# Spreading the merge chain's steps over ticks by weights, asking earlier for a group's inputs, and ranking the second tile in fewer ticks

## The chip, the cores and the metric

The kernel runs on one core of a Trainium2 chip. The metric is the device time of one execution in microseconds, as the median of several runs. The engines are TensorE (PE; its weight loads are PEld), VectorE (DVE), ScalarE (ACT), GpSimd (POOL) and the queue of SyncE (SP), which here only issues transfers.

## What is computed

One layer of an encoder over nine tiles of 128 tokens (eight of a prompt, one of eight short samples), all in float32. The part that matters here comes after the attention:

```python
def merge(o_sb, o_sw, o_mem, gates, w_o_sb, w_o_sw, w_o_mem, w_out):
    mixed = (gates[..., 0, :] * (o_sb @ w_o_sb) + gates[..., 1, :] * (o_sw @ w_o_sw)
             + gates[..., 2, :] * (o_mem @ w_o_mem))
    return mixed @ w_out

def peer_block(xb, w_q, pk_keys, u_tab, v_tab):
    q = (xb @ w_q).reshape(t, PEER_HEADS, 2, PEER_DHALF)
    s = jnp.einsum('thpd,hpkd->thpk', q, pk_keys).astype(jnp.float32)
    v1, i1 = lax.top_k(s[:, :, 0], PEER_TOPK)
    v2, i2 = lax.top_k(s[:, :, 1], PEER_TOPK)
    ...
    best, flat = lax.top_k(cand, PEER_TOPK)
    ...
    g = jax.nn.softmax(best, axis=-1)
    a = jax.nn.gelu(jnp.einsum('thkd,td->thk', u_tab[idx], xb))
    return jnp.einsum('thk,thkd->td', (g * a).astype(xb.dtype), v_tab[idx])

    x = x + merge(o_sb, o_sw, o_mem, gates, w_o_sb, w_o_sw, w_o_mem, w_out)
    x = x + peer_ffn(rmsnorm(x, norm_ffn), w_peer_q, peer_keys, peer_u, peer_v)
```

Every token picks 16 of 16384 experts in each of 8 heads: 128 experts a token, 128 "slots" a tile.

## The kernel before

Projection and attention fill the first 850 us and stay as they are. The function `experts` does the rest. Its tiles are in three **groups**, `GROUPS = ((0, 1), (2, 3, 4, 5), (6, 7, 8))`.

**The slots.** Seven tiles (`SEQ = (0, 1, 2, 4, 6, 7, 8)`) have their experts fetched row by row. A slot is one indirect gather by POOL (L1458) of one expert row a token into a ring of nine buffers: 8 KB a token (u and v), or 4 KB (u alone, `u_rows`) for tile 1. DVE forms the dot product with the token (L1996), ACT the GELU and the weight (L1751, L1760) and a folded diagonal matrix (`diag`, L1769), and PE adds the weighted v row into its accumulator (L1654). For one slot in four of the first tile ACT and POOL do that (L1775, L1482). For tile 1 nothing is accumulated: POOL writes the weight to a table in HBM (`gates_scratch`, L1471), which a dense pass at the end uses. Tiles 3 and 5 go by that table too. POOL may refill a ring buffer only when its slot is done (for tile 1, when DVE has formed the dot product).

**Ticks.** Two slots are one tick, 64 ticks are one tile, and ticks 0 to 447 run through the seven tiles: tile 0 has ticks 0 to 63, tile 1 has 64 to 127, tile 2 has 128 to 191. Since each tick has two dot products on DVE, a moment of the trace is turned into a tick by counting them (all on L1996).

**The front.** Beside the slots every engine works off a chain of numbered steps, the "front" of a group: 24 units of merge (PE: gate matmul L1522 and value matmul L1532, in `Y` parts; ACT tanh L1685; DVE product and sum L1905 to L1909, called a mix here), then the output projection (PE L1547, DVE L1917), the norm, transposes (L1557), queries (PE L1570, ACT L1706), scores (PE L1584, ACT L1719 to L1724) and, for the group's first tile, the ranking by DVE (`top`, L1805 to L1847, three pieces a head, the third a long one). The class `Front` gives each kind of work its step numbers; `paces()` says how many steps every engine does at each tick. The step numbers set only the order within an engine; semaphores hold what belongs together. The steps of group 1 have ticks 26 to 123, those of group 2 have 128 to 251, both spread evenly.

**Order within a tick.** DVE does the two dot products, then the tick's steps, then a piece of ranking of another tile (`RANKED`) and the addition of equal experts (`merge` on DVE, L1872 to L1881, `MERGED`, for tiles 1, 3 and 5). ACT does the weights and diagonals, then the steps. PE accumulates, then does the steps. POOL does its two gathers, then, from tick 73 on, four scatters in four of every eight ticks (`SPREAD`, third entry). SP isn't held to ticks: it runs ahead until a semaphore stops it.

**Ranking of tile 1.** `RANK_AT[1] = (30, 48)`: the 24 pieces of tile 1 begin at tick 30 and have 48 ticks; its duplicates are added at ticks 57 to 60 and 81 to 84, which follow from the same two numbers.

## Time and profile before

| | us |
|---|---|
| median of 3 runs | 4054.19 |
| the three runs | 4054.07, 4062.14, 4054.19 |
| profiled execution, device time | 4089.85 |
| profiled execution, span of its trace | 4088.0 |
| PE busy | 3374.4 (83%) |
| DVE busy | 2752.4 (67%) |
| POOL busy | 1625.1 (40%) |
| ACT busy | 1009.5 (25%) |
| all transfers | 1248.31 MB, mean 305 GB/s |

PE is the busiest engine over the whole, but a mean over stages with different limits says little. The first 850 us are projection and attention; ticks begin at 1054 us, tick 26 is at 1222 us, tick 64 at 1463 us, tick 128 at 1867 us, tick 256 at 2673 us; the dense pass begins at tick 282. In an answer of the trace the number in square brackets, or after the bar, is the time that the engine sat idle before the instruction, and what ended it. The trace counts two records for one float32 matmul.

### The profile page before, as it was taken

To read this page: it belongs to the slowest core of one execution; us is meant where nothing else is said; L and a number is where in the kernel's file an instruction comes from. 1 tells how busy PE (TensorE), PEld (TensorE's weight loads), DVE (VectorE), ACT (ScalarE), POOL (GpSimd) and SP (SyncE) were. 2 spreads that over 40 slices of the span, in tenths; PEclk is the share of its full clock that TensorE was granted. 3 is DMA by queue.
4 is the path that set the end of the run, shared out by engine and by line. 5 is a ranking of instruction groups with operands and counts; after the bars stand their busy time and mean duration, and the time that the engine had idled before them with its cause. 6 is when DMAs were issued, how large, how long until landed. Compare 5 with 4: busy or idle time off the path is not lost.

```text
span 4088.0 us, 40853 instructions
## 1 busy us (share of the span) xinstructions
PE 3374.4 (83%) x13885; PEld 1890.4 (46%) x13885; DVE 2752.4 (67%) x5752; ACT 1009.5 (25%) x2925; POOL 1625.1 (40%) x1327
## 2 busy tenths in 40 slices
PE   8999898989759997865979878720989999989998
PEld 4545665578423335432333433210555555555554
DVE  2131456611787786676988799779976888866667
ACT  2111557711333321312222232311111111111111
POOL 0000000000455557757557676776333333333332
PEclk9999889999879998887989989865999999999999
DMA  5911320034899976758989999999999999999998
GB/s 184 301 41 52 127 88 22 14 134 152 332 389 407 365 282 245 249 198 347 412 350 393 413 379 348 362 386 359 415 414 414 405 408 414 411 414 411 414 410 353
DMA packets 320096, 1248.31 MB, mean 305 GB/s; under 512 B 40320, under 2 KB 134784, under 8 KB 216064
## 3 DMA queue, kind: packets, MB, share of 16 engines
q0 software_dynamic: 141312, 872.69, 53.9%
q1 hardware_dynamic: 129408, 347.85, 22.6%
q10 hardware_dynamic: 49168, 25.17, 2.1%
q8 instruction: 110, 1.80, 0.2%
...
HBM read 1190.33 MB, written 56.16 MB: 305 GB/s over the span
## 4 chain that ended last, share of the span: by engine, by line
PE 25%; DVE 24%; DMA 17%; issue 5%; POOL 4%; ACT 2%; another core or an unknown queue 1%; SPq 0%; DVEq 0%; ACTq 0%; POOLq 0%
DMA shared<-in_experts_dram 10%; PE ps L1616 8%; DVE ring L1996 8%; PE ps L1522 5%; PE ps L1605 3%; DMA ring<-in_experts_dram,idx 3%; PE ps L1654 3%; DVE o_x L1968 3%; PE ps L1547 2%; PE ps L1532 2%; DMA shared<-gates_scratch 2%; POOL gates_scratch L1471 2%; POOL ring L1458 2%; DMA s<-s_scratch 1%
## 5 line engine op out<-in xcount | busy, mean ns | idle before, releaser
L1458 POOL DMA_INDIRECT ring<-in_experts_dram,idx x768 | 956.8, 1246 | 1787.3 <-DVE o_x L1968 774.2
L1616 PE MATMUL ps<-shared 128*128 128x512 f32 x1536 | 692.0, 601 | 86.4 <-DMA shared<-in_experts_dram 75.6
L1996 DVE CUSTOM_DVE_ANT_0 ring<-ring,xp 128x1024 f32<-128x1024 f32 x512 | 634.4, 1272 | 126.8 <-DMA ring<-in_experts_dram,idx 86.9
L1751 ACT ACTIVATE act_<-hid 128x2 f32<-128x2 f32 x448 | 91.0, 203 | 2138.7 <-DVE hid L1996 2012.6
L1654 PE MATMUL ps<-ring,diag 64*64 64x512 f32 x2816 | 409.6, 696 | 243.9 <-ACT diag L1769 216.0
L1605 PE MATMUL ps<-shared 128*128 128x256 f32 x2048 | 467.1, 381 | 150.7 <-ACT shared L1737 145.2
L1605 PEld LDWEIGHTS ps<-shared 128*128 128x128 f32 x2048 | 391.1, 191 | 260.8 <-issue 205.5
L1968 DVE SCALAR_TENSOR_TENSOR o_x<-ring,wgt,o_x 128x1024 f32<-128x1024 f32 x384 | 491.7, 1280 | 0.1
L1616 PEld LDWEIGHTS ps<-shared 128*128 128x128 f32 x1536 | 290.1, 192 | 423.0 <-issue 405.9
L1996 DVE CUSTOM_DVE_ANT_0 ring<-ring,mixn 128x1024 f32<-128x1024 f32 x384 | 469.6, 1223 | 18.4 <-DMA ring<-in_experts_dram,idx 15.2
L1522 PE MATMUL ps<-shared 128*128 128x256 f32 (+2 forms) x1152 | 411.7, 506 | 38.8 <-DMA shared<-hT_scratch 29.8
L1522 PEld LDWEIGHTS ps<-shared 128*128 128x128 f32 x1152 | 219.9, 196 | 237.2 <-issue 159.9
L1471 POOL DMA_INDIRECT gates_scratch<-gd,spot x256 | 296.3, 1158 | 78.5 <-issue 77.7
L1654 PEld LDWEIGHTS ps<-ring,diag 64*64 64x64 f32 x2816 | 100.5, 148 | 483.6 <-ACT diag L1769 272.5
L319 PE MATMUL ps<-shared,hT 128*128 128x512 f32 (+1 forms) x720 | 284.9, 551 | 1.8 <-DVE mhT L435 1.3
L1570 PE MATMUL ps<-shared 128*128 128x256 f32 (+2 forms) x768 | 274.6, 510 | 8.9 <-ACT gt L1706 3.7
L1947 DVE TENSOR_TENSOR shared<-shared 128x256 f32<-128x256 f32 x128 | 54.1, 423 | 271.5 <-DMA shared<-gates_scratch 270.7
L1760 ACT ACTIVATE wgt<-act_,gw 128x1 f32<-128x1 f32 x896 | 215.2, 287 | 15.8
L1570 PEld LDWEIGHTS ps<-shared 128*128 128x128 f32 x768 | 148.4, 200 | 146.4 <-issue 110.4
L1532 PE MATMUL ps<-o_x,shared 128*128 128x256 f32 (+2 forms) x576 | 204.6, 495 | 0.6 <-DMA o_x<-o_scratch 0.6
L319 PEld LDWEIGHTS ps<-shared,hT 128*128 128x128 f32 x720 | 134.4, 191 | 131.3 <-issue 125.0
L1458 POOL DMA_INDIRECT ring<-in_u_rows_dram,idx x128 | 143.2, 1119 | 118.1 <-DVE hid L1996 73.8
...
## 6 DMA issues: line engine op xcount, KB each, us to landing
shared<-in_u_blocks_dram SPq DMA_DIRECT2D x128, 512.0 KB
shared<-in_experts_dram SPq DMA_DIRECT2D x128, 512.0 KB
...
shared<-gates_scratch SPq DMA_DIRECT2D x128, 192.0 KB
...
```

The lines of the kernel that those rows point to most:

```text
L319: last = nc.tensor.matmul(ps[:, bank(u), 0:n], src[:, k, t * P:(t + 1) * P], w[:, c % 2, k, 0:n], start=(k == 0), stop=(k == KC - 1))
L1458: i = nc.gpsimd.indirect_dma_start(out=row, out_offset=None, in_=A["u_rows"] if valued(j) else A["experts"], in_offset=bass.IndirectOffset ...
L1471: i = nc.gpsimd.indirect_dma_start(out=G_d.rearrange("e (t o) -> (e t) o", o=1), out_offset=bass.IndirectOffsetOnAxis(ap=spot[:, a, j:j + ...
L1522: last = nc.tensor.matmul(ps[:, 4 + u % 2, 0:N].rearrange("p (i t) -> p i t", t=P), w[:, k * P:(k + 1) * P], hx[:, 0:n, k, :], start=(k == ...
L1532: last = nc.tensor.matmul(ps[:, 6 + u % 2, 0:N].rearrange("p (i t) -> p i t", t=P), w[:, k * P:(k + 1) * P], o[:, 0:n, b, k - KC, :], star ...
L1570: last = nc.tensor.matmul(ps[:, 4 + x % 2, 0:N].rearrange("p (i t) -> p i t", t=P), w[:, c:c + P], hx[:, 0:n, k, :], start=(k == 0), stop= ...
L1605: last = nc.tensor.matmul(ps[:, 2 + b % 2, 0:ND * P].rearrange("p (a t) -> p a t", t=P), du[:, b % 3, k, :], hx[:, 0:ND, k, :], start=(k = ...
L1616: last = nc.tensor.matmul(ps[:, BANKS[a] + h, :], given, dv[:, v % 3, h * HB:(h + 1) * HB], start=False, stop=(b == NK - 1), skip_group_ch ...
L1654: last = nc.tensor.matmul(acc[c * HD:(c + 1) * HD, r, :], diag[rows, (by_pe(j) - 1) % 4, :], ring[rows, j % RING, DM + c * HB:DM + (c + 1) ...
L1760: last = nc.scalar.activation(wgt[:, i:i + 1], act_[:, i:i + 1], ACT.Copy, scale=gw[:, n % 2, i:i + 1])
L1968: last = nc.vector.scalar_tensor_tensor(out=x1, in0=ring[:, j % RING, DM:2 * DM], scalar=wgt[:, j % SLOTS:j % SLOTS + 1], in1=x1, op0=ALU. ...
L1996: last = nc.vector.tensor_tensor_reduce(out=u, in0=u, in1=rows, scale=1.0, scalar=0.0, op0=ALU.mult, op1=ALU.add, accum_out=hid[:, j % SLO ...
```

## The change

Three things. `LEADS = (0, 2, 6)` puts two empty steps before the units of group 1 and six before those of group 2; SP's requests for the group's inputs stand at step 0 as before. `weight()` gives every step of groups 0 and 1 a weight by its kind (a unit part of group 1 has 2.67, an output step 3.6, a query part 4.8), and `spend` hands out the steps of group 1 to ticks by these weights; group 2 is the last one and has weight 1.0 for all steps. `RANK_AT[1]` becomes (28, 34): tile 1 is ranked at ticks 28 to 61, and its duplicates are added at ticks 48 to 51 and 65 to 68.

```diff
--- before.py
+++ after.py
@@ -1010,6 +1010,9 @@
     return PE_UPTO[j + 1]
 
 
+LEADS = (0, 2, 6)
+
+
 class Front:
 
 
@@ -1019,14 +1022,15 @@
         self.cols = n * P
         self.units0, self.tiles0 = 3 * KC * g, sum(len(x) for x in GROUPS[:g])
         self.outs0, self.q0, self.s0 = 4 * self.tiles0, 2 * PH * g, PH * g
-        self.out_at = 3 * KC * Y + 3
+        lead = self.lead = LEADS[g]
+        self.out_at = lead + 3 * KC * Y + 3
         ends = [self.out_at + 3 * n + i for i in range(n)]
         self.q_at = ends[-1] + 10
         soon = 2 if g == 0 else 0
         self.steps = self.q_at + 4 * PH + 12
-        self.unit = {u * Y + y: (u, y) for u in range(3 * KC) for y in range(Y)}
-        self.tanh = {u * Y + Y + 1: u for u in range(3 * KC)}
-        self.mix = {u * Y + Y + 2: u for u in range(3 * KC)}
+        self.unit = {lead + u * Y + y: (u, y) for u in range(3 * KC) for y in range(Y)}
+        self.tanh = {lead + u * Y + Y + 1: u for u in range(3 * KC)}
+        self.mix = {lead + u * Y + Y + 2: u for u in range(3 * KC)}
         self.out = {self.out_at + i: (i // n, i % n) for i in range(4 * n)}
         self.res = {self.out_at + i + 2: (i // n, i % n) for i in range(4 * n)}
         self.square, self.mean, self.root, self.norm, self.turn, self.keep = (
@@ -1045,6 +1049,19 @@
         self.far = tuple(range(self.base + 2, self.base + n))
         self.far0 = PH * sum(len(x) > 2 for x in GROUPS[:g])
 
+    def weight(self, tau):
+        if self.final:
+            return 1.0
+        if tau < self.lead:
+            return 3.0
+        if tau in self.unit:
+            return 8.0 * self.n / self.Y / 3
+        if tau in self.out:
+            return 3.6
+        if tau in self.query:
+            return 1.2 * self.n
+        return 3.5 if tau >= self.q_at else 1.5
+
 
 FRONTS = [Front(g) for g in range(len(GROUPS))]
 FIRST_OF = {f.base: f for f in FRONTS}
@@ -1075,19 +1092,24 @@
     total = [sum(f.steps for f in FRONTS[:g + 1]) for g in range(len(GROUPS))]
     done = FRONTS[0].first_head
     out = [done]
-    start, mid = done, total[0]
-    for i in range(2 * NB):
-        if i < RANK_LEAD:
-            to = start + -(-(mid - start) * (i + 1) // RANK_LEAD)
-        else:
-            to = min(total[1], mid + -(-(total[1] - mid) * (i + 1 - RANK_LEAD) // (2 * NB - 4 - RANK_LEAD)))
+
+    def spend(f, at, first, last):
+        weights = [f.weight(tau) for tau in range(f.steps)]
+        reached = [sum(weights[:tau + 1]) / sum(weights) for tau in range(f.steps)]
+        for i in range(first, last):
+            share = min(1.0, (i + 1 - first) / (last - 4 - first))
+            yield at + sum(x <= share + 1e-9 for x in reached)
+
+    start = done
+    for i in range(RANK_LEAD):
+        to = start + -(-(total[0] - start) * (i + 1) // RANK_LEAD)
         out.append(to - done)
         done = to
-    mid = done
-    for i in range(2 * NB, DENSE_AT):
-        to = min(total[2], mid + -(-(total[2] - mid) * (i + 1 - 2 * NB) // (G2_TICKS - 4)))
-        out.append(to - done)
-        done = to
+    for f, first, last in ((FRONTS[1], RANK_LEAD, 2 * NB), (FRONTS[2], 2 * NB, 4 * NB)):
+        for to in spend(f, total[f.g - 1], first, last):
+            out.append(to - done)
+            done = to
+    out.extend([0] * (DENSE_AT - 4 * NB))
     ticks = len(SEQ) * NB - DENSE_AT
     for i in range(ticks):
         to = total[2] + -(-DENSE_STEPS.steps * (i + 1) // ticks)
@@ -1098,7 +1120,7 @@
 
 PACES = paces()
 
-RANK_AT = {1: (30, 48), 3: (2 * NB + 2, 28), 4: (2 * NB + 34, 28), 5: (2 * NB + 66, 28), 7: (4 * NB + 8, 36), 8: (5 * NB + 6, 48)}
+RANK_AT = {1: (28, 34), 3: (2 * NB + 2, 28), 4: (2 * NB + 34, 28), 5: (2 * NB + 66, 28), 7: (4 * NB + 8, 36), 8: (5 * NB + 6, 48)}
 RANKED = {at + length * c // (3 * PH): (m, c // 3, c % 3) for m, (at, length) in RANK_AT.items() for c in range(3 * PH)}
 SHIFTED, EXPOSED, WEIGHED = ({at + length * (i + 1) // 2 + lag: (m, 4 * i, 4 * i + 4) for m, (at, length) in RANK_AT.items() for i in range(2)}
                              for lag in range(3))
```

What stands on which tick follows from the tables:

| | before | changed |
|---|---|---|
| group 1, unit parts | ticks 26 to 81 | ticks 27 to 74 |
| group 1, output projection (PE) | 83 to 92 | 75 to 85 |
| group 1, transposes | 94 to 96 | 86 to 87 |
| group 1, queries | 98 to 116 | 88 to 116 |
| group 1, ranking of tile 2 | 103 to 121 | 96 to 121 |
| tile 2's experts chosen and weighed | 122 | 123 |
| tile 1, ranked | 30 to 77 | 28 to 61 |
| tile 1, duplicates added | 57 to 60, 81 to 84 | 48 to 51, 65 to 68 |
| group 2, unit parts | 128 to 190 | 133 to 194 |
| group 2, queries | 213 to 240 | 215 to 241 |
| tile 6's experts chosen and weighed | 250 | 251 |

**PE at the start of group 1.** The row with x64 or x72 is accumulation of tile 0 up to tick 26; in the changed kernel L1654, L1522 and L1532 are L1676, L1544 and L1554. Before:

```order
L1654 MATMUL ps<-ring,diag 64x512 x64
L1522 MATMUL ps<-shared 128x512 x6
L1654 MATMUL ps<-ring,diag 64x512 x8
L1522 MATMUL ps<-shared 128x512 x2
L1532 MATMUL ps<-o_x,shared 128x512 x4
L1654 MATMUL ps<-ring,diag 64x512 x4
```

Changed:

```order
L1676 MATMUL ps<-ring,diag 64x512 x72
L1544 MATMUL ps<-shared 128x512 x3
L1676 MATMUL ps<-ring,diag 64x512 x4
L1544 MATMUL ps<-shared 128x512 x5
L1554 MATMUL ps<-o_x,shared 128x512
L1676 MATMUL ps<-ring,diag 64x512 x8
```

The first unit (12 matmuls) begins one tick later, with one part where there were two, and later units come closer together.

**DVE at the last unit of group 1.** Before, ticks 82 and 83 (L1996 is a dot product, L1872 to L1881 add duplicates, L1907 and L1909 are the mix of the last unit):

```order
L1996 ISA ring,hid<-ring,xp 128x1024
...
L1877 TENSOR_TENSOR work<-number 128x1024
L1879 TENSOR_TENSOR work<-work,raw 128x1024
L1880 TENSOR_REDUCE partf<-work 128x16
...
L1996 ISA ring,hid<-ring,xp 128x1024
...
L1907 SCALAR_TENSOR_TENSOR gt<-gt,ps 128x512
L1909 TENSOR_TENSOR mixn<-mixn,gt 128x512
```

Changed, tick 74 and the start of 75 (L2018 is the dot product, L1929 and L1931 the mix):

```order
L2018 ISA ring,hid<-ring,xp 128x1024
L2018 ISA hid 128x1
L1929 SCALAR_TENSOR_TENSOR gt<-gt,ps 128x512
L1931 TENSOR_TENSOR mixn<-mixn,gt 128x512
L2018 ISA ring,hid<-ring,xp 128x1024
```

The additions of duplicates no longer stand between the last units' mixes; they stand at ticks 65 to 68, where mixes of earlier units are.

## Rows read from the trace of the kernel before

**Rows 1.** The page's slices, 102 us each: busy tenths, and GB/s of all transfers

```profile
PE   8999898989759997865979878720989999989998
DVE  2131456611787786676988799779976888866667
POOL 0000000000455557757557676776333333333332
```

**Rows 2.** Windows (stretch, length, busy and count by engine, granted clock, DMA share, GB/s)

```profile
1225.00:1463.00 238.00, 222.04 (x798) 81.47 (x795) 180.67 (x382) 72.17 (x198) 128.50 (x90) 0.97 0.95 372
1463.00:1557.00 94.00, 93.14 (x240) 40.00 (x238) 73.87 (x179) 21.10 (x67) 59.05 (x49) 1.00 0.72 255
1557.00:1578.00 21.00, 0.42 (x1) 0.45 (x2) 18.18 (x30) 2.74 (x10) 16.43 (x16) 0.53 1.02 404
1664.00:1803.00 139.00, 128.92 (x368) 63.31 (x368) 95.93 (x274) 27.46 (x90) 90.91 (x86) 0.96 0.65 223
1803.00:1867.00 64.00, 10.75 (x32) 7.13 (x32) 42.22 (x112) 13.68 (x44) 33.18 (x29) 0.59 0.65 234
1867.00:2673.00 806.00, 639.05 (x3176) 277.94 (x3176) 672.68 (x1777) 222.00 (x743) 551.84 (x491) 0.90 0.96 379
```

**Rows 3.** Waits, 1225 to 1463 us: who waited for whom, us, times, longest

```profile
POOL ring L1458 <- PE ps L1654: 83.0, 29, 6.5
DVE gt L1907 <- ACT gt L1685: 35.2, 7, 8.7
PE ps L1654 <- ACT diag L1769: 16.0, 7, 5.4
```

**Rows 4.** PE's timeline at tick 26 (start, length, line, shapes, count, idle before)

```profile
1223.27 1.98 PE L1654 MATMUL ps<-ring,diag 64*64 64x512 f32 x8 [1.05 <-ACT diag L1769]
1225.18 6.46 PE L1522 MATMUL ps<-shared 128*128 128x512 f32 x12
```

**Rows 5.** PE's timeline around the last unit of group 1, ticks 80 to 83

```profile
1545.68 7.03 PE L1522 MATMUL ps<-shared 128*128 128x512 f32 x16
1552.55 3.60 PE L1532 MATMUL ps<-o_x,shared 128*128 128x512 f32 x8
1577.58 2.90 PE L1547 MATMUL ps<-shared,mixn 128*128 128x256 f32 x6 [21.44 <-DVE mixn L1909]
```

**Rows 6.** DVE's timeline, ticks 81 to 83

```profile
1561.35 1.22 DVE L1879 TENSOR_TENSOR work<-work,raw 128x1024 f32<-128x1024 f32 x1
...
1568.30 1.22 DVE L1877 TENSOR_TENSOR work<-number 128x1024 f32<-128x1024 f32 x1
...
1576.03 0.68 DVE L1907 SCALAR_TENSOR_TENSOR gt<-gt,ps 128x512 f32<-128x512 f32 x1
1576.74 0.69 DVE L1909 TENSOR_TENSOR mixn<-mixn,gt 128x512 f32<-128x512 f32 x1
```

**Rows 7.** Groups of POOL, 1517 to 1709 us (count, busy, mean ns, idle before)

```profile
L1458 POOL DMA_INDIRECT ring<-in_u_rows_dram,idx x64 | 74.3, 1161 | 26.3 <-issue 17.6 <-DVE hid L1996 8.7
L1471 POOL DMA_INDIRECT gates_scratch<-wgt,spot x64 | 73.8, 1154 | 19.5 <-issue 18.9 <-ACT wgt L1760 0.6
```

**Rows 8.** Waits of POOL, 1709 to 1860 us

```profile
POOL ring L1458 <- DVE hid L1996: 48.7, 15, 9.3
```

**Rows 9.** POOL's timeline: start of the scatters, one gather alone, two beside dot products

```profile
1516.93 0.94 POOL L1458 DMA_INDIRECT ring<-in_u_rows_dram,idx  x1 [1.81 <-DVE hid L1996]
...
1840.13 0.94 POOL L1458 DMA_INDIRECT ring<-in_u_rows_dram,idx  x1 [0.30 <-issue]
...
1857.68 2.00 POOL L1458 DMA_INDIRECT ring<-in_u_rows_dram,idx  x1 [0.31 <-DVE hid L1996]
1859.98 1.96 POOL L1458 DMA_INDIRECT ring<-in_experts_dram,idx  x1 [0.30 <-DVE hid L1996]
```

**Rows 10.** DVE's timeline: the first dot product of tick 128

```profile
1867.01 1.23 DVE L1996 CUSTOM_DVE_ANT_0 ring<-ring,xp 128x1024 f32<-128x1024 f32 x1 [2.14 <-DMA ring<-in_experts_dram,idx]
```

**Rows 11.** DVE's timeline: a long ranking piece of tile 1, first and last row, next dot

```profile
1308.04 0.41 DVE L1814 TENSOR_TENSOR work<-v 128x256 f32<-128x256 f32 x1
...
1316.27 1.23 DVE L1996 CUSTOM_DVE_ANT_0 ring<-ring,xp 128x1024 f32<-128x1024 f32 x1
```

**Rows 12.** PE's timeline, end of group 1 and start of group 2

```profile
1814.89 3.44 PE L1584 MATMUL ps<-shared,gt 128*128 128x128 f32 x16 [12.44 <-ACT gt L1706]
1848.13 2.29 PE L1522 MATMUL ps<-shared 128*128 128x384 f32 x3 [29.80 <-DMA shared<-hT_scratch]
```

**Rows 13.** Groups of PE, 1578 to 1664 us, and 1664 to 1867 us

```profile
L1547 PE MATMUL ps<-shared,mixn 128*128 128x256 f32 x256 | 62.4, 403 | 24.9 <-DVE mixn L1909 21.4 <-issue 3.3
...
L1570 PE MATMUL ps<-shared 128*128 128x512 f32 x256 | 116.4, 612 | 7.3 <-ACT gt L1706 3.7 <-issue 2.4 <-ACT shared L1700 1.2
```

## The prediction

> **What bounds the kernel now.** I read the page's slices first, then windows cut where the work of group 1 changes, then in each window who waits for whom, and last the timelines of the engine that nobody keeps waiting. The slices [rows 1] show PE near full from slice 13 on, but a mean hides which engine is late, and the change touches only ticks 26 to 251 (1222 to 2673 us), so the reading stays there.
>
> Ticks 26 to 81 are TensorE's. In 1225 to 1463 it is busy for 222.0 of 238 us and in 1463 to 1557 for 93.1 of 94 [rows 2]; POOL waits 83.0 us there for PE's accumulation, and DVE waits 35.2 us for a tanh that itself waits for PE [rows 3]. PE waits only 16.0 us for diagonals. DVE's idle time in this stretch is slack.
>
> Then PE stands still for 21.4 us [rows 5]: the output projection at tick 83 needs the last unit's mix, which DVE does only after its dot products and two additions of duplicates at ticks 81 and 82 [rows 6]. From tick 73 (1517 us) another engine is late too: POOL does 64 gathers and 64 scatters from 1517 to 1709 us with 8.7 us of waiting for dots [rows 7]. Ticks 98 to 117 (1664 to 1803 us) are PE's again, 128.9 us busy of 139 [rows 2]: eight heads' queries are squeezed into 19 ticks. POOL gets time to spare (48.7 us of waits for dots [rows 8]). What follows, 1803 to 1867 us, is a tail: PE busy 10.8 us, DVE 42.2, POOL 33.2 of 64 [rows 2]. From 1867 to 2673 us, PE, DVE and the transfers are all near full (639, 673 of 806 us, DMA share 0.96) [rows 2].
>
> **The change, group 1.** No instruction is added or taken away; everything is order. Work it out from 1222 us, where tick 26 begins in both.
>
> Start. The two empty steps take no wait away: the inputs are there when PE comes, since it goes from its accumulation straight into the first unit with no idle time noted [rows 4]. So PE starts two parts late: x12 records in 6.46 us now, which move behind the next tick's accumulation. PE loses 6 to 7 us, bounded by zero (if the next ticks come so much sooner) and by 9 (three parts).
>
> Units. A unit costs PE 7.03 + 3.60 us, 10.3 us from start to start where nothing comes between [rows 5]. Between 1225 and 1463 us, 38 ticks, PE accumulates for the rest of its time, about 1.5 us a tick. Before, 1.75 of a unit's four parts stand on a tick: 4.6 + 1.5 = 6.1 us a tick (measured 238 / 38 = 6.3). Changed it is 2 parts: 5.2 + 1.5 = 6.7. The sum over all 24 units is the same, and PE is the bound in both, so the last unit ends at 1556 + 7 = 1563 us, but at **tick 74, not 81**. DVE must keep up. Its ranking of tile 1 now has 34 ticks for 24 pieces instead of 48; a head is about 8.2 us for the long piece [rows 11] and some 3 us for two short ones. Ticks 28 to 63 thus get about a third more of it, 27 us, on top of 180.7 busy us in 238 [rows 2]. With 6.7 us a tick that is about 5.5 on average, under PE's 6.7. I cost it at nothing: what covers it is DVE's wait for tanh [rows 3]. If that cover fails, see the third rival.
>
> The stall. The duplicates are done by tick 68 and the last mix stands directly behind the dot products of tick 74. Tanh and mix are about 2 us (two DVE rows of 0.7 us [rows 6] and one ACT row), so 21.4 us of PE idle time shrink to 3 to 5. Were PE still the bound, that would be a gain of 17 us less the 7 us of the start. But what is late next is POOL.
>
> POOL. Its scatters stay on ticks 73 and later, and by the structure of units DVE reaches tick 73 when unit 21 is done by PE and mixed: 1563 - 20.6 + 6 = 1548 us, where it was 1517 [rows 9]. From there to the gather of tile 2's first slot POOL has 206 transfers (half and half, the number between 1517 and 1860 us). In its full stretch one takes (74.3 + 17.6 + 73.8 + 19.5) / 128 = **1.45 us**, issue time included [rows 7]. So 206 x 1.45 = 298 us, to 1846; 7 us from issue to the dot product, as now (1859.98 to 1867.01 [rows 9, 10]), make 1853. Waits of POOL come on top: between 0 and the 57 us that it has now (8.7 + 48.7 [rows 7, 8]). I take 6, near the lower end, because what makes them now is gone: the queries get 28 ticks instead of 19, in which DVE has 28 x 2.4 + 8 x 11.5 = 160 us of dots and ranking, PE 116.4 + some 18 us [rows 13], and POOL 120 x 1.45 = 174 us. POOL is the largest of the three, if not by much. The first dot product of tick 128 comes at **1859 instead of 1867 us: 8 us sooner**.
>
> Does PE hold this? 1563 + 4, output projection 62.4 us [rows 13], some 16 us for norm and transposes, 134 for queries and scores: 1779, before tick 117 by POOL's clock. Yes.
>
> **The change, group 2.** In the kernel before, the first part of unit 0 waits 29.8 us for its inputs, but nobody waits for PE then: it had run ahead of the ticks, and its accumulation of tick 128 comes only after the dots at 1867 us [rows 10, 12]. So the six empty steps remove a wait that costs nothing. They give ticks 128 to 132 less PE work (5 us each of transfers and dots go on) and put 146 steps where 140 were: 1.22 a tick instead of 1.17, 0.05 x 2.7 = 0.1 us of PE a tick, in a stretch where PE is busy 79% [rows 2]. From 0 to 6 us lost; up to 5 gained if the ring refills sooner at tick 128. I take zero. Tile 6's experts are ready one tick later, at 251, where POOL asks for them after PE has accumulated slot 503 of the same tick, so after DVE has done it. Zero. From tick 256 on nothing is moved.
>
> **A rule weighed.** POOL's gather takes 0.94 us alone and 2.00 or 1.96 beside dot products that follow each other closely [rows 9]. The Trainium skill, GPSIMD Engine Reference, Specifications, says that GpSimd shares its SBUF interface with VectorE and is held up by VectorE instructions with two SBUF inputs, as a dot product is. The trace agrees. Taken to its end for a POOL that never rests, 41% of its transfers (2.44 us of dots in a tick of 5.9) at 2.0 us and the rest at 0.95 would be 1.38 + 0.30 us, 206 of them 346 us, and tick 128 would come 40 us later than forecast. But the 128 transfers of [rows 7] lived beside just that share of dots and had a mean of 1.16; the measurement decides, and 1.45 stands.
>
> **Rivals.**
> 1. *POOL is quicker.* Beside light DVE work a transfer is 0.94 + 0.30 us [rows 9], and the mean from 1709 to 1860 us is (151 - 48.7) / 78 = 1.31. At 1.35, 206 take 278 us, and the gain is 25 or more: 4029. For it: DVE's ranking reads mostly one input. Against: dots come as densely as in [rows 7].
> 2. *POOL keeps waiting.* If DVE's long pieces still come in clumps, POOL's waits are 15 to 20 us, not 6, and tick 128 stays where it is: 4054 to 4058. For it: DVE's 160 us and POOL's 174 are close, and the ring holds only four ticks.
> 3. *DVE stalls PE in ticks 28 to 74, slower.* In twelve units instead of eight tanh and mix stand on the same tick, and DVE must wait there for ACT, which waits for PE, before it does the dots that PE's next accumulation needs. With a long piece in between: 2.4 + 1.4 + 8.2 = 12 us, and 3 us to the diagonals, against 6.7 us of PE work a tick. PE's waits for diagonals, 16.0 us now [rows 3], would grow by up to 4 us for each of eight long pieces. Every microsecond delays tick 73 and with it the whole chain of POOL. It decides from 8 us on (no gain left); at 24 us the time is 4070.
> 4. *Group 2 pays.* The units squeezed into fewer ticks run into a stretch in which three resources are nearly full; 10 us are lost there: 4064 without the gain of group 1, 4056 with it.
>
> **How the numbers follow.** The profiled span is 4088.0 us; the change makes it 4080. The median of the runs shown is 4054.19, 0.8% lower; 8 us less of it is 4046. A measurement of this kernel can tell about 0.2% (8 us) from no change, so this forecast sits on that edge. Chances: forecast 0.45 (own range 4038 to 4054; 0.27 of it under 4046), rival 1 0.17 (4029), rival 2 0.15 (4056), rival 3 0.15 (4070), rival 4 0.08 (4064). Faster 0.27 + 0.17 = 0.44, within 0.2% 0.18 + 0.15 = 0.33, slower 0.23. The range 4022 to 4070 leaves out the far part of rival 1 and the worse half of rival 3.
>
> **What would show it.** Last unit's value matmul of group 1 ending at 1558 to 1568 us (right), later than 1575 (rival 3, with PE's waits for diagonals over 25 us before it). Idle time of PE before the output projection 3 to 5 us. The first scatter near 1550 us. From there to 1855 POOL's waits for dots under 10 us and 1.45 us a transfer; over 20 us of waits is rival 2, under 1.38 us a transfer rival 1. First dot of tick 128 at 1859. From there to tick 256, 806 us as before; 812 or more is rival 4. Tick 256 to the end unchanged (1415 us). I'd be wrong in the mechanism if POOL were idle for long in ticks 76 to 120.

## The result, and the profile after

| | before | changed |
|---|---|---|
| median, us | 4054.09 (5 runs, 4050.39 to 4062.14) | **4081.99** (5 runs, 4076.14 to 4086.99) |
| ratio, 95% interval | | **1.0066** [1.0048, 1.0084] |
| profiled execution, device time | 4089.85 | 4076.14 |
| its span | 4088.0 | 4074.3 |

The changed kernel is slower by 28 us, where I forecast 8 us faster. The two profiled executions say the contrary (14 us less), since the one of before lies 36 us above the median of its kernel and the one of after 6 us below. The profile of before is none of the five runs in the table, and the record does not say on which chip it was taken. On the four chips of the experiments the medians of this same kernel were 4104 to 4117 us, 50 to 62 us above 4054, so the 36 us may be a difference of chips; no run here settles it. So I took the pair again, both on one chip, `c0_before` and `c1_after`, and every ratio below is against runs of the kernel before on the same chip. For each stage I give both executions where I have two. Two executions, one of `g2_ceil` with 7776 us and one of `dup_after` with 16736 us, are slow ones and are in no ratio below.

The page's slices of the changed kernel (102 us each, as [rows 1]):

```profile
PE   8999898989658998855889878720999899889988
DVE  2131446611787966687988799779976788766667
POOL 0000000000454446777567766776333333333332
```

Windows of the changed kernel, as [rows 2] (length, busy and count of PE, PEld, DVE, ACT, POOL; granted clock, DMA share, GB/s): ticks 26 to 73, 73 to 104, 104 to 128, 128 to 256.

```profile
1215.00:1553.00 338.00, 311.93 (x1027) 118.38 (x1028) 266.64 (x562) 89.36 (x244) 157.98 (x115) 0.95 0.85 319
1553.00:1725.00 172.00, 149.92 (x514) 95.38 (x513) 106.56 (x233) 42.90 (x133) 135.12 (x120) 0.93 0.79 276
1725.00:1858.00 133.00, 62.73 (x190) 32.09 (x188) 108.21 (x293) 29.59 (x98) 104.47 (x94) 0.74 0.75 262
1858.00:2660.00 802.00, 639.51 (x3192) 278.54 (x3192) 672.22 (x1777) 221.05 (x743) 550.33 (x490) 0.89 0.96 381
```

Waits in it from tick 26 to the end of the last unit (1215 to 1566 us), as [rows 3]:

```profile
POOL ring L1480 <- PE ps L1676: 127.1, 40, 8.1
DVE gt L1929 <- ACT gt L1707: 36.0, 11, 6.6
DVE mixn L1927 <- ACT gt L1707: 22.8, 5, 5.9
PE ps L1676 <- ACT diag L1791: 21.5, 6, 6.1
PE ps L1544 <- ACT gt L1707: 7.3, 1, 7.3
```

The last line is new: PE's matmuls of a unit waiting for ACT's tanh. PE's timeline at ticks 68 to 75, the counterpart of [rows 5], shows where it stands:

```profile
1531.89 3.60 PE L1554 MATMUL ps<-o_x,shared 128*128 128x512 f32 x8
1542.78 9.45 PE L1544 MATMUL ps<-shared 128*128 128x512 f32 x16 [7.29 <-ACT gt L1707]
...
1562.36 3.60 PE L1554 MATMUL ps<-o_x,shared 128*128 128x512 f32 x8
1568.32 3.91 PE L1569 MATMUL ps<-shared,mixn 128*128 128x256 f32 x17 [2.37 <-DVE mixn L1931]
```

and DVE's timeline beside it, with ACT's tanh (one row of ACT):

```profile
1517.74 1.22 DVE L2018 CUSTOM_DVE_ANT_0 ring<-ring,xp 128x1024 f32<-128x1024 f32 x1
...
1523.01 0.17 DVE L1894 COPY gw<-raw 128x16 f32<-128x16 f32 x1
...
1529.33 1.22 DVE L2018 CUSTOM_DVE_ANT_0 ring<-ring,xp 128x1024 f32<-128x1024 f32 x1
...
1531.61 0.17 DVE L1894 COPY gw<-raw 128x16 f32<-128x16 f32 x1
...
1538.73 1.22 DVE L2018 CUSTOM_DVE_ANT_0 ring<-ring,xp 128x1024 f32<-128x1024 f32 x1
```

```profile
1541.95 0.69 ACT L1707 ACTIVATE gt<-ps,bgh 128x512 f32<-128x512 f32 x1
```

These are ticks 67 and 68. Between the dots at 1517.74 and 1529.33, and again up to 1538.73, stand the additions of one head's duplicates (L1894 to L1903), 6.4 and 7.2 us, and the ticks take 11.6 and 9.4 us where PE has some 5 us of work, two parts of a unit. Ticks 65 to 68 together take 40.8 us, with DVE busy for 33.3 of them. A tick's tanh stands behind the same tick's GELU in ACT's order, and that waits for the dots. So the tanh of a unit whose matmuls ended at 1535.5 comes at 1541.95, PE finds no free PSUM half (units write two halves in turn, and a tanh frees its own), and stands still for 7.3 us. So in ticks 65 to 68 DVE was the bound, in the middle of the units.

The page's marks of the forecast: last unit's end 1566.0 (forecast 1558 to 1568), stall before the output projection 2.37 us (3 to 5), tick 73 at 1553 (1548 to 1550), first dot of tick 128 at 1858 (1859), span 4074 (4080). In this one execution nearly all of it came as forecast; the median of the kernel did not. That is what the experiments had to settle.

### The profile page after: what moved, and what is told of

It reads as the page before. It is cut to its first block, busy times and chain, and to the rows that moved or that the text cites. A ratio compares the mean times of both kernels' runs of the same rounds, so it can differ in the third digit from the quotient of the medians.

```text
span 4074.3 us, 40849 instructions
## 1 busy us (share of the span) xinstructions
PE 3362.0 (83%) x13885; PEld 1882.0 (46%) x13885; DVE 2757.1 (68%) x5752; ACT 1004.0 (25%) x2920; POOL 1620.9 (40%) x1327
## 4 chain that ended last, share of the span: by engine, by line
PE 25%; DVE 21%; DMA 20%; POOL 7%; issue 5%; ACT 1%; SPq 0%; DVEq 0%; ACTq 0%; POOLq 0%
DMA shared<-in_experts_dram 11%; PE ps L1638 8%; DVE ring L2018 7%; PE ps L1544 5%; DMA ring<-in_experts_dram,idx 5%; POOL gates_scratch L1493 4%; PE ps L1627 4%; POOL ring L1480 3%; PE ps L1676 3%; PE ps L1554 3%; DVE o_x L1990 2%; DMA shared<-gates_scratch 2%; PE ps L1592 1%; DVE work L1851 1%; PE ps L1569 1%
## 5 line engine op out<-in xcount | busy, mean ns | idle before, releaser
L1480 POOL DMA_INDIRECT ring<-in_experts_dram,idx x768 | 945.3, 1231 | 1805.2 <-DVE o_x L1990 772.5
L2018 DVE CUSTOM_DVE_ANT_0 ring<-ring,xp 128x1024 f32<-128x1024 f32 x512 | 627.1, 1255 | 169.6 <-DMA ring<-in_experts_dram,idx 107.9
L1676 PE MATMUL ps<-ring,diag 64*64 64x512 f32 x2816 | 416.6, 711 | 252.8 <-ACT diag L1791 252.6
L2018 DVE CUSTOM_DVE_ANT_0 ring<-ring,mixn 128x1024 f32<-128x1024 f32 x384 | 469.4, 1222 | 17.8 <-DMA ring<-in_experts_dram,idx 14.7
L1544 PE MATMUL ps<-shared 128*128 128x256 f32 (+2 forms) x1152 | 406.2, 501 | 11.8 <-ACT gt L1707 7.3
L1676 PEld LDWEIGHTS ps<-ring,diag 64*64 64x64 f32 x2816 | 101.2, 151 | 498.5 <-ACT diag L1791 326.3
L1544 PEld LDWEIGHTS ps<-shared 128*128 128x128 f32 x1152 | 217.5, 194 | 207.7 <-issue 157.7
L1592 PE MATMUL ps<-shared 128*128 128x256 f32 (+2 forms) x768 | 275.5, 510 | 25.9 <-ACT gt L1728 23.4
L1554 PE MATMUL ps<-o_x,shared 128*128 128x256 f32 (+2 forms) x576 | 201.8, 492 | 0.6 <-DMA o_x<-o_scratch 0.6
L912 DVE SCALAR_TENSOR_TENSOR sps<-ps,za 128x512 f32<-128x512 f32 x76 | 52.3, 688 | 199.1 <-ACT za L878 199.1
## 6 DMA issues: line engine op xcount, KB each, us to landing
ring<-in_experts_dram,idx POOLq DMA_INDIRECT x768, 12.2
```

What stands on the lines that cost most here:

```text
L1480: i = nc.gpsimd.indirect_dma_start(out=row, out_offset=None, in_=A["u_rows"] if valued(j) else A["experts"], in_offset=bass.IndirectOffset ...
L1544: last = nc.tensor.matmul(ps[:, 4 + u % 2, 0:N].rearrange("p (i t) -> p i t", t=P), w[:, k * P:(k + 1) * P], hx[:, 0:n, k, :], start=(k == ...
L1554: last = nc.tensor.matmul(ps[:, 6 + u % 2, 0:N].rearrange("p (i t) -> p i t", t=P), w[:, k * P:(k + 1) * P], o[:, 0:n, b, k - KC, :], star ...
L1592: last = nc.tensor.matmul(ps[:, 4 + x % 2, 0:N].rearrange("p (i t) -> p i t", t=P), w[:, c:c + P], hx[:, 0:n, k, :], start=(k == 0), stop= ...
L1676: last = nc.tensor.matmul(acc[c * HD:(c + 1) * HD, r, :], diag[rows, (by_pe(j) - 1) % 4, :], ring[rows, j % RING, DM + c * HB:DM + (c + 1) ...
L2018: last = nc.vector.tensor_tensor_reduce(out=u, in0=u, in1=rows, scale=1.0, scalar=0.0, op0=ALU.mult, op1=ALU.add, accum_out=hid[:, j % SLO ...
```

## Experiments

All ratios are against the kernel before on the same chip, with a 95% interval, from 6 to 12 runs of each version. Two ratios that come from different chips are compared as ratios only. `RANK_AT[1]`, `LEADS` and `weight` are the names of the diff. A wait "at tick N", here and in the expectations, lies just before the first dot of tick N: the one "at tick 118" stands between the first dots of ticks 117 and 118.

### The parts one by one

> The kernel before, unchanged. Its one profiled execution shown so far (4089.85 us) is 36 us above its median, while the changed kernel's median is 28 us above it and its profiled execution 14 us below. Theory A (the order theory): executions of the kernel before spread, the usual one reaches tick 128 at about 1830 us and not at 1867; a second profile then reads 4055 to 4065 us. Theory B: profiling itself adds some 35 us to this kernel and not to the changed one; a second profile reads about 4090 with tick 128 at 1867 again, and the median of its plain runs stays at 4054.

> The changed kernel, unchanged. Both theories: 4076 to 4087 us in plain runs, ratio 1.005 to 1.009, and a profile with tick 64 near 1493 us, tick 73 near 1555, tick 128 near 1858 and tick 256 near 2660, 803 us after it.

`r_only`, the kernel before with the ranking's numbers alone:

```diff
-RANK_AT = {1: (30, 48), ...
+RANK_AT = {1: (28, 34), ...
```

> The kernel before with the ranking table's entry alone changed: tile 1 is ranked at ticks 28 to 61, duplicates added at 48 to 51 and 65 to 68; leads and weights are not there. If the denser ranking costs (rival 3 of the prediction): PE's waits for diagonals in ticks 28 to 64 go from 16 us to over 25 and the time is 4065 or more. If it is free, the 21 us of PE's idle time before the output projection go down to 3 to 8 us and the time is 4035 to 4054.

`a_oldrank`, the changed kernel without them:

```diff
-RANK_AT = {1: (28, 34), ...
+RANK_AT = {1: (30, 48), ...
```

> The changed kernel with the old entry of the ranking table (30, 48): leads and weights alone. If the late arrival at tick 73 and the full GpSimd queue behind it cost the 28 us, it is as slow as the changed kernel or slower (4078 to 4095), since the last unit still stands at tick 74. If the ranking was the cost, it is 4050 to 4065.

| | ratio | 95% |
|---|---|---|
| `c0_before` | 0.9998 | [0.9982, 1.0015] |
| `c1_after` | 1.0047 | [1.0030, 1.0064] |
| `r_only` | 1.0056 | [1.0036, 1.0076] |
| `a_oldrank` | 0.9977 | [0.9960, 0.9994] |

Neither theory on the 36 us holds. The second profile of before is 4099.70 us, 14 us under the median of its kernel on that chip, so profiling does not add some 35 us; and tick 128 comes at 1880.6 us, so on that chip it is not the quick execution that theory A expects either. `c1_after` has a ratio just under the range I gave, and its ticks 128 and 256 come at 1894 and 2715 us, not at 1858 and 2660.

Taking the ranking's numbers back gives back the whole loss: they cost 0.56% in the kernel before, and 0.70% (29 us) between `a_oldrank` and the changed kernel. The rest of the change gains 0.2%. Where the ranking costs it, PE's windows from tick 26 (its first dot, 1218.4 us in the profile of before, not the 1222 us given ahead of the prediction) to the end of the last unit's value matmul show. Each has the same 1056 records. In this order: before, `c0_before`, changed, `c1_after`, `a_oldrank`, `r_only` (length, PE busy, clock, DMA share, GB/s):

```profile
1218.00:1556.00 338.00, 320.46 (x1056) 0.97 0.88 341
1215.00:1555.00 340.00, 320.32 (x1056) 0.97 0.88 339
1215.00:1566.00 351.00, 324.89 (x1056) 0.95 0.85 319
1219.00:1566.00 347.00, 324.29 (x1056) 0.95 0.86 323
1231.00:1553.00 322.00, 315.62 (x1056) 0.99 0.91 345
1225.00:1581.00 356.00, 326.86 (x1056) 0.95 0.84 323
```

Two executions of one kernel agree here within 3 us, so this stretch can be read from one profile. The 28 us between `a_oldrank` and the changed kernel (322.6 and 350.6 us before rounding) are 17.5 us of PE's waits (11.3 and 28.8) and 9.3 us of PE's own busy time for the same matmuls, at a mean granted clock of 0.99 and 0.95 of the upper level (2.4 GHz). Where PE waited more, its clock was lower too, and the longer busy time came to half of the waits again.

How far that reaches, the same executions show further on (us from the first dot of tick 26; the last column is the stretch behind it):

| | last unit ends | output projection starts | tick 128 | ticks 128 to 256 |
|---|---|---|---|---|
| before | 337.8 | 359.2 | 648.6 | 806.5 |
| `c0_before` | 340.0 | 361.7 | 665.4 | 803.8 |
| changed | 350.6 | 353.0 | 642.5 | 802.5 |
| `c1_after` | 347.7 | 350.1 | 675.6 | 820.7 |
| `a_oldrank` | 322.6 | 325.0 | 655.4 | 820.0 |
| `r_only` | 356.7 | 376.3 | 687.3 | 812.3 |

Four of these ran on one chip (`c0_before`, `c1_after`, `a_oldrank`, `r_only`). There the ranking costs 20 us up to tick 128 (`a_oldrank` to `c1_after`) and 22 us (`c0_before` to `r_only`). Against before, though, the changed kernel is not late at the output projection: its units take some 10 us more and the stall behind them is 19 us shorter. What `c1_after` loses on `c0_before` comes after that: it is 10 us behind at tick 128 and loses 17 us more up to tick 256. The 17 us are not the ranking's, since `a_oldrank` has them too. And the changed kernel's two executions are 33 us apart at tick 128, so one profile of each does not say where behind the units a loss lies.

`w_only` has weights, no leads (`LEADS = (0, 0, 0)`) and the old ranking; `lead_only` the leads, the old ranking and even steps, by this edit (the lines behind the new `return` stay and are never reached):

```diff
     def weight(self, tau):
-        if self.final:
-            return 1.0
+        return 1.0
```

> Weights alone: the changed kernel with no empty steps (leads 0, 0, 0) and the old ranking entry (30, 48). Leads and weights together measured 0.9977 of before. Theory W (the weights gain by putting the last unit at tick 74, so that PE goes into the output projection at once; the leads cost a little): 0.993 to 0.997. Rival L (the leads carry the gain): 0.998 to 1.002.

> Leads alone: two and six empty steps, all steps spread evenly, old ranking entry. Theory W: nobody waits for the inputs that the leads give time to, so nothing is gained and up to 15 us are lost: 1.000 to 1.004; ticks 128 to 256 take up to 15 us longer in the profile. Rival L: 0.996 to 0.999.

Measured: `w_only` 0.9992 [0.9975, 1.0008], `lead_only` **0.9929 [0.9903, 0.9955]**. My theory that the weights bring the gain and the leads cost fell. Windows of `w_only`, then of `lead_only`, each for ticks 26 to 73, 73 to 104 and 104 to 128:

```profile
1216.00:1519.00 303.00, 300.66 (x1025) 115.35 (x1026) 250.33 (x497) 86.45 (x244) 157.50 (x116) 0.99 0.94 358
1519.00:1719.00 200.00, 153.08 (x506) 96.57 (x505) 136.79 (x298) 46.69 (x135) 137.79 (x125) 0.87 0.69 235
1719.00:1855.00 136.00, 70.33 (x209) 36.37 (x207) 107.41 (x292) 29.36 (x98) 97.77 (x89) 0.76 0.73 255
```

```profile
1227.00:1519.00 292.00, 276.13 (x953) 103.20 (x954) 232.62 (x495) 84.94 (x241) 161.28 (x117) 0.96 0.94 367
1519.00:1697.00 178.00, 133.37 (x444) 86.16 (x443) 120.83 (x226) 45.27 (x125) 133.62 (x114) 0.86 0.70 249
1697.00:1860.00 163.00, 107.49 (x333) 54.95 (x331) 126.24 (x367) 35.94 (x114) 110.22 (x98) 0.86 0.70 240
```

With the weights PE is done with the units 316.4 us after tick 26, 21 and 24 us sooner than in the two executions of before, and the output projection follows at once. The ticks gain less. Against `lead_only`, tick 73, where POOL's scatters begin, comes 303 us after tick 26 and not 291, because there is more of PE's work ahead of it, and 73 to 128 takes 336 us where `lead_only` takes 341. Against before, tick 128 does come sooner, 638.7 us after tick 26 where the two executions of before have 648.6 and 665.4. But ticks 128 to 256 then take 829 us in place of 806.5 and 803.8, although no weight and no lead of `w_only` is in group 2. That is the rounding of a later section, and there the gain of the weights went.

### How long the ranking may be

`rank41` is the kernel before with `RANK_AT[1] = (29, 41)`; `w_rank28` is `w_only` with (28, 46).

> The kernel before with tile 1's ranking at ticks 29 to 69 (41 ticks instead of 48; the changed kernel has 34, which alone cost 0.56%). If the cost is the density of ranking on DVE beside the units (a dose), it lies between: 1.001 to 1.004, PE's waits for diagonals in ticks 26 to 64 between 26 and 37 us. If the cost is one collision of the entry (28, 34) with the units, 41 ticks cost nothing: 0.998 to 1.001.

> Weights alone with the ranking at ticks 28 to 73 (46 ticks), so that the first four heads' duplicates are added by tick 57 and GpSimd's gather of tile 1's first slot no longer waits 9 us for them. If that wait mattered it is 2 to 8 us under the run with weights alone; if PE is the bound there, as I read it, it is the same within 3 us, or up to 5 us slower for the denser ranking.

Measured: `rank41` **0.9955 [0.9939, 0.9972]**, `w_rank28` 1.0006 [0.9987, 1.0025], which the noise does not tell from `w_only`. The theory of a dose (the shorter, the dearer) fell too: 48 ticks 1, 41 ticks faster, 34 ticks slower. PE's timeline in `rank41` around the last unit:

```profile
1558.40 3.60 PE L1532 MATMUL ps<-o_x,shared 128*128 128x512 f32 x8
1566.30 3.94 PE L1547 MATMUL ps<-shared,mixn 128*128 128x256 f32 x11 [4.31 <-DVE mixn L1909]
```

Its units take as long as before (337.8 us), but the second half of the duplicates stands on ticks 73 to 76, not on 81 to 84, and the stall of 21.4 us before the output projection [rows 5] is 4.3: 17 us less, and the ratio is worth 18. That the two numbers agree shows no more than that they agree: at tick 128 this execution is 646.8 us after tick 26, where before has 648.6 and 665.4. In `r_only` these additions stand on ticks 65 to 68 and the stall is still 19.6 us, while the units take 17 to 19 us more. That made the place of the duplicates the suspect, not the length.

### The duplicates' place

`late_dup` is the changed kernel, ranking in 34 ticks, with tile 1's duplicates on the kernel before's ticks. `r_late` is the same on `r_only`. `dup76` is `late_dup` with [57, 76].

```diff
-MERGED = {at + length * (i + 1) // 2 + 3 + h: (m, 4 * i + h) for m, (at, length) in RANK_AT.items() if m in PASSED ...}
+MERGED_AT = {m: [at + length * (i + 1) // 2 + 3 for i in range(2)] for m, (at, length) in RANK_AT.items()}
+MERGED_AT[1] = [57, 81]
+MERGED = {MERGED_AT[m][i] + h: (m, 4 * i + h) for m in RANK_AT if m in PASSED ...}
```

> The changed kernel, with the additions of tile 1's duplicates (one head a tick, some 8 us of VectorE each) put back on ticks 57 to 60 and 81 to 84 while the ranking pieces keep their 34 ticks; with 34 ticks they had moved to 48 to 51 and 65 to 68, between the units. In the changed kernel PE waits 24 to 27 us between ticks 28 and 78 (3.9 us at tick 54, 1.9 at 62, 7.3 at tick 70, right behind the duplicates), with the old ranking only 6 to 8. Theory D (the duplicates' new place makes most of the loss): the waits at ticks 54 to 70 go, 11 to 13 us of PE's waits, the last unit ends that much sooner, and the ratio falls from 1.0047 to 1.001 to 1.002. Rival P (the denser ranking pieces make the loss, wherever the duplicates are): waits of 20 us or more stay, ratio 1.004 to 1.006.

> The kernel before with tile 1's 24 ranking pieces in 34 ticks from 28, as in the run that gave 1.0056, but the additions of duplicates on their old ticks 57 to 60 and 81 to 84. Theory D (the place of the duplicates among the units makes the loss): the waits of 9.2, 5.1 and 2.0 us at ticks 54, 63 and 70 fall to the 5 to 6 us that the kernel before has there, and the ratio is 1.000 to 1.002. Rival P (the denser pieces themselves slow PE in ticks 28 to 48, which took 142 us and not 128 with them): ticks 28 to 48 stay at 140 us, ratio 1.003 to 1.005. I give D the better chance, since the same edit took 0.57% off the changed kernel.

> The changed kernel with the duplicates of heads 0 to 3 on ticks 57 to 60 as before, those of heads 4 to 7 on ticks 76 to 79: right behind the last unit's mix (tick 74), ahead of the output projection's residual additions. Theory D: as good as on ticks 81 to 84 (ratio 0.999) or better by up to 5 us, since VectorE has little at ticks 76 to 79: 0.997 to 0.999, PE's waits between ticks 28 and 78 at 16 us. Rival: they hold up the dots that POOL and PE wait for there, and the ratio is 1.000 to 1.003.

| | ratio | 95% | with the duplicates on 48 to 51 and 65 to 68 |
|---|---|---|---|
| `late_dup` | 0.9990 | [0.9976, 1.0003] | 1.0047 (changed) |
| `r_late` | 1.0003 | [0.9984, 1.0023] | 1.0056 (`r_only`) |
| `dup76` | 1.0013 | [0.9993, 1.0032] | |

The theory holds twice, with 0.57 and 0.53%, each the difference of two ratios from different chips whose intervals lie apart. It is a theory of place, not quite of "among the units": heads 0 to 3 are still among them, on ticks 57 to 60, and the two halves were not moved one by one. PE's windows, tick 26 to the end of the last unit, of `late_dup` and `r_late`:

```profile
1224.00:1559.00 335.00, 320.51 (x1056) 0.97 0.90 336
1230.00:1579.00 349.00, 323.06 (x1056) 0.96 0.87 332
```

and PE's timeline of `late_dup` at the last two units, where the changed kernel stood still for 7.3 us:

```profile
1545.48 3.60 PE L1556 MATMUL ps<-o_x,shared 128*128 128x512 f32 x8
1548.91 7.03 PE L1546 MATMUL ps<-shared 128*128 128x512 f32 x16
1555.78 3.60 PE L1556 MATMUL ps<-o_x,shared 128*128 128x512 f32 x8
1561.74 2.61 PE L1571 MATMUL ps<-shared,mixn 128*128 128x256 f32 x11 [2.37 <-DVE mixn L1933]
```

In `late_dup` PE waits 17.7 us (28.8 and 25.9 in the two executions of the changed kernel), ticks 65 to 68 take 21.4 us and not 40.8, and the units take 335.6 us. In `r_late` the units gain only 7 us on `r_only` (349.8 for 356.7), but tick 128 comes 659.2 us after tick 26 where `r_only` has 687.3. In `late_dup` it comes after 665.2 us, between the changed kernel's 642.5 and 675.6: there the way from the units to the 0.57% is not shown by the profiles. The denser pieces by themselves are not free: in `r_late`, as in `r_only`, ticks 28 to 48 take 141 to 142 us where the kernel before needs 127 and 128; but the ticks after are shorter, since the ranking is done, and the kernel ends even. `dup76` I had expected to be as good as `late_dup` or better. Its units are as quick (335.4 us), but its ratio is not better; in its profile DVE waits 23.8 us for scores at tick 101, which no other run has there, so I can't say what the place costs.

### Leads, and a rounding that I hadn't seen

`lead_rank41` is `lead_only` with (29, 41). `lead_g1` and `lead_g2` are `lead_only` with `LEADS = (0, 2, 0)` and `(0, 0, 6)`.

> Leads (0, 2, 6) with every step spread evenly, and the second tile ranked in 41 ticks from 29. If the two gains have different places (leads: the waits of tick 118 and the refill at 128; 41 ticks: PE's waits between ticks 28 and 78 and the stall before the output projection), they add: 0.9929 x 0.9955 = 0.988, some 4067 us. If both only move the steps to luckier ticks, they don't add: 0.992 to 0.997.

> Even steps, leads (0, 2, 0): group 1 alone starts two steps late. Theory G1 (the leads' gain of 0.7% is in group 1: two steps more shift group 1's queries and rankings against the ticks, and VectorE's wait of 13.9 us for scores at tick 118 is gone, ticks 116 to 118 take 12 us instead of 26): ratio 0.994 to 0.996. Theory G2 (the gain is that tile 2's first ticks are not held up by group 2's inputs, ticks 128 to 136 in 54 us instead of 62): ratio 0.999 to 1.001.

> Even steps, leads (0, 0, 6): group 2 alone has its inputs asked for six steps ahead. Theory G1: ratio 0.998 to 1.000, with ticks 128 to 136 some 8 us shorter and nearly all of it given back by tick 204. Theory G2: ratio 0.993 to 0.995. In both, PE's wait of 29 us for group 2's inputs at tick 123 is gone, and with it nothing if nobody waits for PE there, as I had argued.

Measured: 0.9986 [0.9968, 1.0003], 0.9959 [0.9942, 0.9976] and **0.9940 [0.9917, 0.9963]**. The gains of `lead_only` (0.71%) and `rank41` (0.45%) not only don't add, together they leave nothing clear of noise: the units of `lead_rank41` take 358.9 us with 31.7 us of waits, against 337.8 and 19.9 in `rank41`. Group 1's steps stand one or two ticks later than in `rank41`, and meet the same ranking pieces elsewhere: PE waits at ticks 45, 54, 60 and 77.

Either lead alone gains. Reading the tables for why, I found what the diff holds beside its three parts: the old `paces()` rounds a tick's number of steps up (`-(-x // y)`), the new one counts the steps *reached*, so it rounds down. With no lead and even steps 84 of group 1's 168 steps and 120 of group 2's 140 stand one tick later. That was to be separated:

```diff
 # even0: lead_only with
+LEADS = (0, 0, 0)
 # g2_ceil: lead_g2 with the old rounding, its group 1 is that of before
-            yield at + sum(x <= share + 1e-9 for x in reached)
+            yield at + min(f.steps, -(-f.steps * (i + 1 - first) // (last - 4 - first)))
 # top_late: the kernel before with tile 2's ranking pieces one step later
-        self.top = {self.q_at + 4 * h + 9 - soon + i: ...
+        self.top = {self.q_at + 4 * h + 9 - soon + (g == 1) + i: ...
```

> No leads, even steps, ranking in 48 ticks: what is left of the change is that a tick's number of steps is rounded down in place of up, which puts 84 of group 1's 168 steps and 120 of group 2's 140 one tick later. Theory S (same tick): in the kernel before, six of tile 2's eight heads have VectorE's first ranking piece on the tick of ScalarE's copy of their scores, two with this rounding; VectorE's wait of 13.9 us at tick 118 goes (ticks 116 to 118 in 12 us, not 26), but at tick 195 it waits 15 us for tile 5's scores, not 6 (as in the two kernels with weights and no leads). Ratio 0.995 to 0.998. Theory L (the leads themselves are the gain): ratio 0.999 to 1.001.

> The kernel before with group 2's lead of six steps alone, steps rounded up as before, group 1 untouched. Theory S: the 14 us wait at tick 118 stays, ticks 128 to 136 take 53 us and not 62, half of it is given back by tick 204: ratio 0.997 to 1.000. Theory L: ratio 0.993 to 0.995, as with leads and the other rounding.

> The kernel before with one edit: the three ranking pieces of each head of tile 2 stand one step later in group 1's order, all else on its old tick. Theory S: the same-tick meetings of copy and first piece become fewer, the waits at ticks 106 to 118 (8 to 14 us each) shrink, ticks 104 to 118 take 12 to 20 us less: ratio 0.995 to 0.998. If the waits only move to the next tick: 0.999 to 1.001.

Measured: `even0` 0.9993 [0.9980, 1.0005], `g2_ceil` 1.0012 [0.9997, 1.0026], `top_late` 0.9990 [0.9974, 1.0006]. Neither theory comes through whole. The rounding alone gives nothing, the lead of group 2 alone gives nothing, both together 0.6%. What can be read of it is group 2, ticks 128 to 256, in all runs by these two:

| | steps rounded up | rounded down |
|---|---|---|
| no lead | 804, 807, 812, 812, 815, 815 us | 825, 828, 829, 831 us |
| lead of 6 | 822 us | 803, 812, 814, 815, 816, 816, 820, 821, 822 us |

Rounding down costs group 2 some 18 us where there is no lead, and the lead takes 13 of them back. A part of that has a name. Tile 5's ranking begins at tick 194 with scores that come back from HBM, and SP's load of them stands in its queue behind the requests that follow group 2's last units. In `w_rank28` (rounded down, no lead), SP's rows and the DVE row that waited:

```profile
2287.35 0.33 SPq L1320 DMA_DIRECT2D shared<-in_w_out_dram  x1
2287.72 0.95 SPq L1351 DMA_DIRECT2D o_x<-in_x_prompt_dram  x2
...
2289.25 0.36 SPq L1459 DMA_DIRECT2D s<-s_scratch  x1
...
2310.25 0.29 DVE L1827 MAX8 v<-s 128x8 f32<-128x128 f32 x1 [18.97 <-DMA s<-s_scratch]
```

Here SP gives out the load 1.5 us after the first dot of tick 194, in `c0_before` 10 us before it. The same row of DVE in `c0_before`, `even0` and `lead_g2`:

```profile
2309.64 0.29 DVE L1805 MAX8 v<-s 128x8 f32<-128x128 f32 x1 [5.42 <-DMA s<-s_scratch]
```

```profile
2301.81 0.30 DVE L1826 MAX8 v<-s 128x8 f32<-128x128 f32 x1 [16.41 <-DMA s<-s_scratch]
```

```profile
2285.15 0.29 DVE L1826 MAX8 v<-s 128x8 f32<-128x128 f32 x1 [8.96 <-DMA s<-s_scratch]
```

In group 1 the rounding moves a meeting. In the kernel before, the first ranking piece of six of tile 2's eight heads stands on the same tick as ACT's copy of its scores; at tick 118 DVE then waits for it in every profile with that order:

```profile
1814.38 0.29 DVE L1805 MAX8 v<-s_first 128x8 f32<-128x128 f32 x1 [13.67 <-ACT sst L1724]
```

(13.9, 13.8, 12.2, 13.5 and 13.8 us in `c0_before`, `r_only`, `rank41`, `r_late` and `g2_ceil`.) Rounded down and with no lead before group 1 it is two heads, ticks 116 to 118 take 12 to 15 us and not 26, but `even0` has 18.1 us of the same wait at tick 105 and `top_late`, where no head has the two on one tick, 15.5 at tick 109. `late_dup`, where copy and first piece stand on ticks 116 and 117, has 13.6 us at tick 118 all the same. So the shared tick is not enough to explain the wait. The waits moved rather than went, and the interval of `top_late` holds 1. Why `lead_g2` has 0.5% on `even0`, of which group 2 shows 12 of 22 us, and why two steps before group 1 gain 0.3% on it, **stays open**: the rest falls mostly into ticks 104 to 118, where executions of one kernel differ by as much.

### Behind the last mix

`dup_after` is `lead_g2` with `MERGED_AT[1] = [57, 86]`.

> Even steps, lead of six for group 2, ranking in 48 ticks, and the additions of tile 1's last four heads moved from ticks 81 to 84 to ticks 86 to 89, behind the last unit's mix. Theory D (duplicates between units cost, behind the last mix they don't): PE's wait of 21 to 27 us before the output projection shrinks to 3 to 8, tick 88 comes 12 to 18 us sooner, of which POOL keeps up to a half back: ratio 0.989 to 0.992 (0.994 without that edit). If POOL is the bound there, as I forecast for tick 73 on: ratio 0.993 to 0.995.

Measured: 0.9959 [0.9945, 0.9974], no better than `lead_g2` (0.9940 [0.9917, 0.9963]) and outside the ranges of both theories. Waits of DVE from 1536 to 1566 us, and PE's output projection:

```profile
DVE ring L2019 <- DMA ring<-in_u_rows_dram,idx: 14.2, 6, 4.3
```

```profile
1565.49 20.72 PE L1570 MATMUL ps<-shared,mixn 128*128 128x256 f32 x87 [15.69 <-DVE mixn L1932]
```

With the additions gone from ticks 81 to 84 DVE waits for gathers instead, 14.2 us, and the stall stays at 15.7 us (18.1 in `lead_g2`). Between ticks 73 and 86 POOL waits 0.6 us for dots in all: its gathers and scatters set the pace there, which is the bound that I had forecast behind the duplicates, and it takes up what moving them frees. From tick 86 to 128 it is not the bound alone, since it waits 43 us for dots.

## Why the prediction was wrong

**The step that failed: the ranking costed at nothing.** I averaged the ranking over ticks 28 to 63 and found DVE's 5.5 us under PE's 6.7. Measured, DVE is busy for 5.9 us a tick there and a tick takes 7.4 us (7.0 in `a_oldrank`). The duplicates I only counted as gone from ticks 81 and 82 ("done by tick 68"); where they went, 65 to 68, is among the units, with 6.4 and 7.2 us of additions on a tick beside dots and mixes. No average over 35 ticks shows four that are too long. That, with the pieces' part, is 25 to 28 us of the units' time (28.0 in one pair: 17.5 of waits, 9.3 of longer busy time at a lower clock), 20 us at tick 128 and 0.70% of the kernel (29 us); the duplicates' place alone is worth 0.57%.

**A second term was mis-sized: POOL's waits for dots, 6 us in the sum.** They are 2.8 us in one execution of the changed kernel and 37.3 in the other. They are 45.8 us in `a_oldrank`, so this is not the ranking's doing alone, and what makes them differ between two executions stays open. So `a_oldrank`'s 0.9977, worth 9 us where I forecast 8, is luck and not the sum come true: its tick 73 comes 311 us after tick 26 where the sum has 326, and POOL then waits some 40 us more than the sum has.

**Last unit at 1563 us.** 1566.0 and 1566.4, right by two errors that cancel. "The sum over all 24 units is the same, and PE is the bound in both" was wrong: with the old ranking the same units, spread by weights, take 322.6 and 316.4 us where they took 338, because PE waits less (11.3 and 4.8 us against 20 and 22.5) and its clock is higher. The ranking then costs 25 to 28 us. The mark could not tell this; PE's waits could. I had set "diagonals over 25 us" for rival 3: they are 21.5 and 18.6, and with the wait for ACT's tanh 28.8 and 25.9.

**Start.** A loss of 6 to 7 us forecast; PE stands still for 6.1 us in tick 28 in one execution and 3.2 in the other. Right in the first, half of it in the second.

**Stall.** 2.4 us, forecast 3 to 5. Right in size, and right in cause only in part: it is 2.4 in `late_dup` too, with the duplicates on 81 to 84. What ended it here is that the last mix is on tick 74; in `rank41`, with the last mix on tick 83, moving the duplicates ahead of it did nearly the same (4.3 us).

**POOL.** Groups of POOL in the changed kernel from tick 73 to 128, as [rows 7]:

```profile
L1493 POOL DMA_INDIRECT gates_scratch<-wgt,spot x108 | 124.7, 1155 | 32.9 <-issue 32.6 <-ACT wgt L1782 0.3
L1480 POOL DMA_INDIRECT ring<-in_u_rows_dram,idx x103 | 112.4, 1091 | 31.7 <-issue 28.7 <-DVE hid L2018 2.8 <-DVEq L1889 0.3
```

(124.7 + 112.4 + 32.9 + 28.7) / 211 = 1.42 us a transfer (forecast 1.45), 2.8 us of waits for dots (6), ticks 73 to 128 in 304.7 us (305). But in `c1_after` POOL waits 37.3 us for dots and the stretch takes 340.6. That is rival 2, right in one of the two. The Trainium skill (GPSIMD Engine Reference, Specifications) has GpSimd held up by VectorE instructions with two SBUF inputs. With 1.16 us a scatter and 1.09 us a gather here (1.15 and 1.13 in `c1_after`), the measured mean was again the right price, and what made the difference between the two executions was waiting, not the transfer's length.

**Group 2.** Forecast 806 us and nothing lost; measured 802.5 and 820.7, and 803 to 822 over nine runs with this order, mean 815, against a mean of 811 for the old. Four to five us, which the spread of the two sets does not tell from nothing, so at most a part of rival 4; in the pair on one chip it is 17 us (803.8 and 820.7), more than half of that pair's 31. What I had not read is the rounding in `spend`, which moves 120 of its 140 steps. It is in the diff's text and the order would have shown it.

**From 4080 to 4046.** I took the difference of a sum made on one profiled execution over to the median of others. The profile of before lay 36 us above its kernel's runs and I scaled that gap away as if it were the same for both kernels. Ticks 73 to 128 alone take 352.7 and 367.3 us in two executions of before, 304.7 and 340.6 in two of after: a term of 8 us can't be read off such a stretch.

**Rivals.** Rival 3 (DVE stalls PE in ticks 28 to 74, slower) was the right one in place and in sign. Its size fell short: it has 24 us and 4070 us at the worst, where the ranking costs 29 us and the kernel takes 4082, and its marks did not come (last unit later than 1575, waits for diagonals over 25 us). It named tanh and mix on one tick with a long ranking piece between; the worse half was the duplicates. I had given it 0.15, and its price had no row of the duplicates under it.
